# Two transformer blocks in one kernel: bias tables and a norm's squares moved beside weight chunks, and the modulated operand made by three engines

## The reference

```python
mod = jax.nn.silu(c) @ w_ada[l] + b_ada[l]
shift, scale, gate = jnp.split(mod[:, None, :], 3, axis=-1)
h = rms_norm(x, norm_g[l]) * (1.0 + scale) + shift          # hc likewise, from ctx and c_ctx
(a_glu, a_gate, nq, nk, nv, n_gate, wq, wk, wv, w_gate, merge) = jnp.split(h @ w_in[l], SPLIT_POINTS, axis=-1)
# convolution branch: depthwise convolution of 31 taps, layer norm over 512 channels, silu
# neighbourhood attention with a relative bias table (na_rpb), window attention with a sink
x = x + gate * (sum of three gated branches) @ w_o
```

## Time and profile before

| what | value |
|---|---|
| median of three runs | 2804.88 us |
| profiled execution, its own time | 2804.84 us |
| its span | 2803.1 us |
| PE busy | 2529.4 us, 90% |
| VectorE busy | 1530.3 us, 55% |
| ScalarE busy | 1274.4 us, 45% |
| GpSimd busy | 219.6 us, 8% |
| mean granted clock of TensorE | 0.927 of full speed |

### The profile page before, as it was taken

The page is one execution under the profiler, slowest core; times in us unless marked ns, Lnnn a source line. Parts: engine busy times, 40 slices in busy tenths (PEclk is TensorE's granted clock), DMA queues, the critical chain, the costliest instruction groups (busy, mean ns, idle before and its releaser), DMA issues. The chain is left out here.

```text
span 2803.1 us, 46994 instructions
## 1 busy us (share of the span) xinstructions
PE 2529.4 (90%) x17866; PEld 2276.6 (81%) x17866; DVE 1530.3 (55%) x2701; ACT 1274.4 (45%) x1969; POOL 219.6 (8%) x212
## 2 busy tenths in 40 slices
PE   6897679999889689959998999899999989898998
PEld 4676458887678579949996879899999977798998
DVE  4488553334558555625556555555555454655554
ACT  5364553232546454414345454543443454544433
POOL 0022000000003000002100000022021000000220
PEclk8999899999989799979996789999999976999999
DMA  8221022222532025435532214455355432153552
GB/s 333 103 94 45 14 91 91 91 104 90 210 120 95 24 91 185 176 114 183 190 140 101 96 70 180 141 184 186 136 187 187 142 128 76 67 190 136 179 180 105
DMA packets 60996, 368.56 MB, mean 131 GB/s; under 512 B 5888, under 2 KB 18224, under 8 KB 18352
## 3 DMA queue, kind: packets, MB, share of 16 engines
q1 hardware_dynamic: 60704, 366.49, 36.5%
q10 hardware_dynamic: 144, 0.01, 0.0%
HBM read 359.10 MB, written 7.37 MB: 131 GB/s over the span
## 5 line engine op out<-in xcount | busy, mean ns | idle before, releaser
L210 DVE TENSOR_TENSOR w_lo<-ring,w_hi 128x1024 fp32r<-128x1024 f32 x652 | 819.9, 1299 | 547.0 <-ACT w_hi L198 547.0
L252 PE MATMUL psum<-x_hi,w_hi 128*128 128x256 f32 (+1 forms) x3392 | 1041.0, 307 | 66.4 <-DVE x_lo L570 21.9
L253 PE MATMUL psum<-x_lo,w_hi 128*128 128x256 f32 (+1 forms) x3392 | 1032.0, 304 | 0.0
L254 PE MATMUL psum<-x_hi,w_lo 128*128 128x256 f32 (+1 forms) x3392 | 1031.5, 304 | 0.0
L198 ACT ACTIVATE w_hi<-ring 128x1024 fp32r<-128x1024 f32 (+1 forms) x652 | 653.4, 1050 | 356.3 <-PE psum L254 154.2
L252 PEld LDWEIGHTS psum<-x_hi,w_hi 128*128 128x128 f32 x3392 | 659.3, 194 | 103.1 <-issue 58.4
L253 PEld LDWEIGHTS psum<-x_lo,w_hi 128*128 128x128 f32 x3392 | 659.8, 195 | 24.0 <-issue 1.4
L254 PEld LDWEIGHTS psum<-x_hi,w_lo 128*128 128x128 f32 x3392 | 659.3, 194 | 23.3
L1553 PE MATMUL psum<-h_hi,w_hi 128*128 (+1 forms) x640 | 181.1, 283 | 0.0
L1555 PE MATMUL psum<-h_lo,w_hi 128*128 (+1 forms) x640 | 181.1, 283 | 0.0
L1556 PE MATMUL psum<-h_hi,w_lo 128*128 (+1 forms) x640 | 181.1, 283 | 0.0
(11 more groups left out here) (275 smaller groups left out, 3202.6 us busy)
## 6 DMA issues: line engine op xcount, KB each, us to landing
ring<-wstream SPq DMA_DIRECT2D x327, 1024.0 KB, 4.8
kept_hi<-x_hi SPq DMA_DIRECT2D x1, 2048.0 KB, 6.3
kept_lo<-x_lo SPq DMA_DIRECT2D x1, 2048.0 KB, 13.0
x_hi<-kept_hi SPq DMA_DIRECT2D x1, 2048.0 KB, 7.8
x_lo<-kept_lo SPq DMA_DIRECT2D x1, 2048.0 KB, 12.5
near<-bias_by_distance SPq DMA_DIRECT2D x2, 1024.0 KB, 7.5
na_bias<-rpb SPq DMA_DIRECT2D x4, 438.0 KB, 5.7
cst<-consts SPq DMA_DIRECT2D x1, 1662.0 KB, 10.5
```

The source lines that it names most:

```text
L210: dve.tensor_tensor(w_lo[:, c % 2, h], ring[:, (c + 2 * i) % RING, h], w_hi[:, c % 2, h].bitcast(F32), ALU.subtract).then_inc(split_done.s ...
L252: pe.matmul(o, w_hi[:, c, w_cols], hi, start=first, stop=False)
L253: pe.matmul(o, w_hi[:, c, w_cols], lo, start=False, stop=False)
L254: return pe.matmul(o, w_lo[:, c, w_cols], hi, start=False, stop=last)
```

## The change

The new parts, by stage:

- `ada_stage`: its loops are written out. ScalarE squares x two tiles at a time beside chunks 8 to 11, and PE sums them a chunk later, into another bank of psum. In layer 0 x and the context are loaded behind chunks 2 and 3 of the loop, the vectors and constants behind 5 and 6, block 2's table and buckets behind 7.
- `mod_stage`: takes the inverse root and multiplies x by it (128x512). In layer 0 it also makes the product of table and buckets and writes it to memory.
- `model_norm`: ScalarE scales and shifts (two activations a tile), GpSimd rounds 128x512, VectorE subtracts 128x512. The first glu chunk is worked through with both tiles side by side.
- `conv_norm_stage` takes the place of `halve_stage` with `norm_of` and of the bias stage in `attend_near`: one stage, with the bias table requested at its head.
- `merge_stage` of the last layer splits x into the right half of x_hi and x_lo beside the out chunks (`halves`).
- `RelBias` in the first `ffn_stage`: the table is read at its head, six flips stand behind chunk 1 and two behind chunk 3. The read of the compressed keys' part falls away, it is taken from the flipped table.

```diff
-        def mod_stage(mod, rows, layer):
+        def mod_stage(mod, rows, layer, scratch, tables):
...
+                    if layer == 0:
+                        sp.wait_ge(read.sem, read.n + 2)
+                        sp.dma_start(table, tables[2][:]).then_inc(loaded.sem, 16)
+                        sp.wait_ge(loaded.sem, lb + 16)
...
+                    if layer == 0:
+                        pe.matmul(psum[0:2 * HEADS, 2048:2048 + 511], tables[0][:], tables[1][:], start=True, stop=True
+                                  ).then_inc(read.sem, 1)
...
+                    inverse_root(act, psum[:, 1024:1024 + 2 * S], rs[:], eps_col, r0)
...
+                    dve.wait_ge(rooted.sem, r0 + 2)
+                    for k in range(KT):
+                        dve.tensor_tensor(scratch(k), x[:, k, :], rs[:], ALU.mult).then_inc(scaled_x.sem, 1)
...
                     for j in range(n):
                         load_one(sp, j // 2, j % 2)
+                        if j == 2:
+                            sp.dma_start(x[:, :, 0:S], xT).then_inc(stored.sem, 16)
+                        if j == 3:
+                            sp.dma_start(x[:, :, S:2 * S], ctxT).then_inc(stored.sem, 16)
+                        if j == 5:
+                            sp.dma_start(vec[:], vecs).then_inc(loaded.sem, 16)
                         if j == 6:
-                            sp.dma_start(vec[:], vecs).then_inc(loaded.sem, 16)
+                            sp.dma_start(cst[:], consts[:, 0:N_RESIDENT]).then_inc(loaded.sem, 16)
...
-                    each_chunk(pe, n, chunk)
+                    for j in range(n):
+                        chunk(j // 2, j % 2)
+                        for k in range(2 * (j - first - 1), 2 * (j - first)):
+                            if k >= 0:
+                                sum_squares(pe, k)
+                    for k in range(2 * (n - first - 1), KT):
+                        mm = sum_squares(pe, k)
...
+                        for k in range(2 * (j - first), 2 * (j - first) + 2):
+                            if k >= 0:
+                                act.activation(scratch(k), x[:, k, :], ACT.Square).then_inc(squared.sem, 1)
...
             def act_steps(act):
                 for k in range(KT):
+                    act.wait_ge(scaled_x.sem, s0 - KT + k + 1)
+                    for w in range(2):
+                        v = scratch(k)[:, w * S:w * S + S]
+                        o = act.activation(v, v, ACT.Identity, scale=scales[:, k, w:w + 1], bias=mod[:, k, w:w + 1])
+                    o.then_inc(mixed.sem, 1)
+                round_next(act, 0, 0)
+
+            def pool_steps(pool):
                 for k in range(KT):
+                    pool.wait_ge(mixed.sem, m0 + k + 1)
+                    pool.tensor_copy(x_hi[:, k, :], scratch(k)).then_inc(upper.sem, 1)
...
+                for k in range(KT):
+                    dve.wait_ge(upper.sem, u0 + k + 1)
+                    dve.tensor_tensor(x_lo[:, k, :], scratch(k), x_hi[:, k, :].bitcast(F32), ALU.subtract
+                                      ).then_inc(lower.sem, 1)
                 rest_next(dve, 0, 0)
...
+        def conv_norm_stage(layer, tok, src, scratch, na_bias, jobs):
...
+                    for k in range(nt):
+                        mm = pe.matmul(psum[:, 0:tok], ones, src[:, k, 0:tok], start=k == 0, stop=k == nt - 1)
+                    mm.then_inc(step.sem, 1)
+                    pe.wait_ge(loaded.sem, lb + 32)
+                    for h in range(6):
+                        mm = turn_round(h)
+                    mm.then_inc(parted.sem, 1)
+                    for k in range(nt):
+                        pe.wait_ge(squared.sem, q0 + k + 1)
+                        mm = pe.matmul(psum[:, 512:512 + tok], ones, scratch[:, k, 0:tok], start=k == 0,
+                                       stop=k == nt - 1)
+                    mm.then_inc(step.sem, 1)
+                    for h in range(6, HEADS):
+                        pe.wait_ge(mixed.sem, m0 + h - 5)
+                        mm = turn_round(h)
+                    mm.then_inc(parted.sem, 1)
...
+                    dve.wait_ge(rooted.sem, r0 + 2)
+                    for k in range(nt):
+                        dve.tensor_tensor(src[:, k, 0:tok], src[:, k, 0:tok], rs[:, 0:tok], ALU.mult
+                                          ).then_inc(scaled_x.sem, 1)
+                    lower_part(1)
+                    dve.wait_ge(parted.sem, f0 + 2)
+                    for h in range(6, HEADS):
+                        bias_of(h)
+                    dve.memset(na_bias[:, NA_COLS:], 0.0)
...
+            def x_upper(act, j, i):
+                m = slice(2 * i, 2 * i + 2)
+                act.wait_ge(acc_free.sem, g0[0] + j)
+                act.activation(x_hi[:, m, S:], x[:, m, 0:S], ACT.Copy).then_inc(upper.sem, 1)
...
+        class RelBias:
...
+            def pe(self, pe, part):
+                pe.wait_ge(loaded.sem, self.lb + 32)
+                for k in (range(6), range(6, 8))[part]:
+                    if part:
+                        pe.wait_ge(mixed.sem, self.m0 + k - 5)
+                    mm = pe.matmul(self.bank(k), const("flip"), rel_bias[:, 2 * k:2 * k + 2, :], start=True, stop=True)
+                mm.then_inc(parted.sem, 1)
...
-        rel_bias_stage()
-        split_stage(x[:, :, 0:S], x_hi[:, :, 0:S], x_lo[:, :, 0:S])
         for layer in range(DEPTH):
-            ffn_stage(layer, layer_norm(layer - 1, 3) if layer else None)
+            ffn_stage(layer, layer_norm(layer - 1, 3) if layer else None, bias=None if layer else RelBias())
```

More of the change, by code:

```diff
@@ L355, in _ @@
                     mm.then_inc(step.sem, 1)
+                    if layer == 0:
+                        pe.matmul(psum[0:2 * HEADS, 2048:2048 + 511], tables[0][:], tables[1][:], start=True, stop=True
+                                  ).then_inc(read.sem, 1)
+                @block.scalar
+                def _(act):
+                    inverse_root(act, psum[:, 1024:1024 + 2 * S], rs[:], eps_col, r0)
+                    if layer == 0:
+                        act.wait_ge(read.sem, read.n + 1)
+                        act.activation(tables[2][:], psum[0:2 * HEADS, 2048:2048 + 511], ACT.Copy).then_inc(read.sem, 1)
                 @block.vector
@@ L369, in _, with ada_stage @@
                                               None, ALU.mult)
-            step.n += 3
-        def ada_stage(c_both, rows, layer):
+                    dve.wait_ge(step.sem, b + 2)
+                    dve.tensor_tensor(mod[:], v[:, :, 2:4], mod[:], ALU.add).then_inc(step.sem, 1)
+                    dve.wait_ge(step.sem, b + 3)
+                    dve.scalar_tensor_tensor(out=scales[:], in0=mod[:, KT:2 * KT, :], scalar=1.0,
+                                             in1=par(layer, "norm_g").unsqueeze(2).to_broadcast([P, KT, 2]),
+                                             op0=ALU.add, op1=ALU.mult)
+                    dve.wait_ge(rooted.sem, r0 + 2)
+                    for k in range(KT):
+                        dve.tensor_tensor(scratch(k), x[:, k, :], rs[:], ALU.mult).then_inc(scaled_x.sem, 1)
+            step.n += 3
+            rooted.n += 2
+            scaled_x.n += KT
+            if layer == 0:
+                read.n += 2
+                loaded.n += 16
+        def ada_stage(c_both, rows, layer, scratch, tables):
             n = ADA_CHUNKS
             b = step.n
+            q0, x_loaded = squared.n, stored.n + (32 if layer == 0 else 0)
+            first = 8
             with nc.Block() as block:
@@ L577, in layer_norm @@
             return Norm(None, act_steps, dve_steps, lambda pe, k: pe.wait_ge(lower.sem, l0 + k + 1))
-        def split_stage(src, hi, lo):
-            b = step.n
-            with nc.Block() as block:
-                @block.scalar
-                def _(act):
-                    act.activation(hi, src, ACT.Copy).then_inc(step.sem, 1)
-                @block.vector
-                def _(dve):
-                    dve.wait_ge(step.sem, b + 1)
-                    dve.tensor_tensor(lo, src, hi.bitcast(F32), ALU.subtract).then_inc(step.sem, 1)
-            step.n += 2
@@ L912, in _ @@
                                                ).then_inc(upper.sem, 1)
+                        if halves and kind == "out" and i:
+                            x_upper(act, j, i - 1)
                         if kind in ("gate", "merge"):
@@ L988, in _ @@
                                 y_lower(2, slice(6, 8))
+                        if halves and kind == "out" and i:
+                            x_lower(dve, i - 1)
                         if kind == "out":
                             take_out(dve, j, i)
+                    if halves:
+                        x_lower(dve, OUT_CHUNKS - 1)
                     if moments:
@@ L1112, in _ @@
                     pool.memset(cpad[:, :, :, PAD + S:], 0.0)
+                    norm.pool(pool)
                 @block.vector
@@ L1486, in ffn_stage @@
```

(14 more changed lines are left out.)

427 lines of the change are left out of this document (184 added, 243 removed).

## The result

The changed kernel takes 2723.66 us (median of four runs, 2719.38 to 2729.70); the kernel before ran beside it at 2805.70 (four runs, 2802.95 to 2808.51). The ratio is 0.9709 (0.9685 to 0.9734), so 82 us less; forecast were 76.5. The profiled execution took 2719.38 us, 85.5 less than the one before. Five more runs, in another session (last experiment), gave 2736.05 (ratio 0.9753). Both lie within the range, and the difference between the sessions is explained under "the hardware".

The account below looks back on a forecast made before the run. PE, busy 90% of the span, bounds the kernel, so gains come only where it stands still. Terms 34.3 + 25.5 + 10.2 + 6.5 = 76.5 us took 2804.8 to 2728 us; range 2712 to 2744.

Parts of the forecast that it names:

- between the blocks: Between block 1 and block 2: removing the table and rounding stage saves 41.5 us, flips cost 7.2, net 34.3 us.
- convolution norm and near bias: From the convolution's norm to near attention: requesting the bias table at stage opening saves 12.2 and 13.3 us, together 25.5.
- norm, layer 0: Norm ahead of layer 0's first projection: first glu chunk ends at 81.2 instead of 91.4, saving 10.2 us (6 to 14).
- norm, layer 1: Norm ahead of layer 1's first projection: chunk 1 starts at 787.1 instead of 793.6, saving 6.5 us (2 to 10).
- Rival (c): In the ffn, tables land late or VectorE's adds starve PE: up to 10 us wait at chunk 2, 2738 us; chance 0.05.
- with the same bytes in all; so I expect chunk 12 near 50 ... and the last two sums until 55.5: Layer 0's ada stage: reordered loads bring chunk 12 near 50, sums end at 55.5, block opens at 56, 2.4 us later.
- on the loads if layer 0's transposes start after 58: Sign in layer 0's norm: transposes starting after 58 would show the forecast wrong on the loads.
- ada of layer 1 should be some 3 us longer up to chunk 11: Sign in layer 1's ada stage: it should take some 3 us longer up to chunk 11.
- a step is 0.7 + 0.69 + 0.05 = 1.45: In the norms: GpSimd's round and VectorE's subtract cannot overlap, so each step takes 1.45 us; bounds 0.91 and 4.3.
- What a step costs: In the norms: GpSimd and VectorE lock each other out of a shared port, so a step is their sum, 1.45 us.
- Rival (d): In the norms: GpSimd's round beside VectorE makes the kernel slower, losing 76.5 us at 6.2 us a step; chance 0.02.
- Rival (b): Whole kernel: more is won, with no GpSimd and VectorE hindrance, early loads, warm PE: 88 us, 2717 us; chance 0.11.

Follow-up runs that it names:

- last experiment: The changed kernel run once more unchanged (e11), beside another run of e6's kernel on one chip: 2736.05 us against 2717.43 us.
- e4: Changed kernel with the stage between the blocks (bias tables, flips, adds, split of x) put back: 2758.24 us.
- e7: Changed kernel with the convolution's norm and the neighbourhood bias in two stages again, table requested at the head of the second: 2750.54 us.
- e1: Changed kernel with the loads of block 2's table and buckets on a count of their own: 2725.92 us, ratio 0.9711.
- e2: Kernel before the change, with only the ada stages' hardware loops written out: 2796.86 us, ratio 0.9974.
- e10: Changed kernel with each of GpSimd's rounds made twice, one after the other: 2737.85 us, one run.
- e9: Changed kernel with the multiplies by the root between VectorE's subtracts and the root in psum: 2722.15 us, one run.
- e3: Changed kernel with the norm's operand made as before by VectorE and ScalarE in 256 columns, GpSimd idle: 2721.61 us.
- e5: Changed kernel with multiplies between VectorE's subtracts, table loads counted apart and SyncE's wait for the written table moved to RelBias: 2719.92 us.
- e11: The changed kernel once more, nothing different, in another session: 2736.05 us, ratio 0.9753.
- e6: Changed kernel with the operand by VectorE and ScalarE, table loads counted apart and SyncE's wait for the written table moved: 2715.47 us.

## Why the prediction was right, step by step

| term | forecast | measured |
|---|---|---|
| between the blocks | 34.3 | 43.3 - 6.9 = 36.4 in the profile; 34.6 by e4 |
| convolution norm and near bias | 25.5 | 13.3 + 14.2 = 27.5 in the profile, 26.4 of them in the stage itself; 26.9 by e7 |
| norm, layer 0 | 10.2 | 3.7 |
| norm, layer 1 | 6.5 | 13.4 |
| not in any term | 0 | 4.5, of which 3.9 are one stage of block 2 at another clock |

**Between the blocks**: right. One rounding and one subtract after the last take_out took until 1148.65, and PE began at 1149.12, 1.9 us after the take_out ended; I had 1.8. Chunk 0 took 6.0 us instead of the 7.8 that I kept from the slow clock, and that is the surplus. It is partly luck: in e1, with the same instructions there, chunk 0 took 7.5 at a granted clock of 0.82. The length before also varies, 52.06 us in its profile and 48.35 in e2, so the term is 32.7 to 36.4. The flips cost 6.9 (forecast 7.2). VectorE's adds were hidden: chunk 3's split began at 1169.65, and chunks 2 and 3 are read 5.76 us apart. Rival (c) did not come.

**Convolution norm**: right. Layer 0's table landed 7.1 us after its request, 0.85 after the sums. In layer 1 PE waited 4.92 for it, as I had said.

**Norm, layer 0**: the step "with the same bytes in all; so I expect chunk 12 near 50 ... and the last two sums until 55.5" failed, and not in its first half, since chunk 12 is rounded at 50.43. I counted bytes and did not ask what the first sums wait for. They wait for all four small loads, the bucket's among them, which landed 10.5 us after its issue. The block opened at 64.05 instead of 56: 5.5 of these 8.05 us are that wait, for without it the root starts at 58.55 (e1). Most of the rest is seen in e1 too: 3.60 us of sums behind the last chunk, four tiles, where I had two. My sign for it, "on the loads if layer 0's transposes start after 58", showed (64.07). From root to read it took 23.8 us, where I had 25.2.

**Norm, layer 1**: undersized by 6.9 us, in two terms of about the same size: the block opened 3.5 us earlier after the last take_out than I had, and root to read was 3.2 us shorter. I set the loops' unrolling against a table load and so at nothing; the chunks now come in pairs of 5.0 us where the hardware loop needed 5.65, and e2 measures 3.0 us for it. So my sign "ada of layer 1 should be some 3 us longer up to chunk 11" failed: it was 0.4 longer. And "a step is 0.7 + 0.69 + 0.05 = 1.45" was 1.01; from the first subtract's end to the last one's were 7.4 us, where seven steps of 1.45 are 10.2, so 2.7 less. The bound beside that term was mis-added as well: with steps of 0.91 its own sum gives 10.3, not 9.6.

**What a step costs**: the mechanism, exclusion, was right, the size was wrong. A cast alone took 0.61 us (I took 0.7), a subtract alone 0.69, but 0.14 and 0.15 us of these are beginning and end, which may overlap with the other; exclusive are 0.47 and 0.54. The Trainium skill, in "SBUF — State Buffer", section "SBUF: two separate sides", says that the two block each other fully, each for the whole instruction, and share no bandwidth. The traces agree but for the 0.14 us at the ends: every subtract that begins within a cast ends 0.54 us after it, e10's second cast puts 0.56 on every step, and with an input of psum (e9) nothing is blocked. In the changed kernel the exclusion costs little, since ScalarE's 0.98 a tile (I had 0.91) would pace the steps without it. What the changed kernel loses to two engines (e3, 2.2 us a layer) is the order, eight multiplies ahead of everything else; the price of the exclusion shows where the order is mended, 2.2 us between e5 and e9. Rival (d) was far off, since no cast took over 1.1 us; nor was any as long as the 1.4 that I gave for one beside a subtract.

The two norm terms were 16.7 together and came out at 17.1, by two errors that cancel. The total says nothing of either, and that it came out so near is in this part luck. Rival (b) had the two large terms almost exactly (36 and 28) and overrated the norms (24). My "about 0.2% (5.6 us)" for what a measurement can tell was too small: two medians of the changed kernel lie 12.4 us apart.

## What to carry to other kernels

When loads move to another place, look up for each what counts it and who waits for that count: an early consumer that waits for a shared count waits for the last load in it. A stage worth moving is one in which PE stands for a transfer or for one short operation; put beside weight chunks, it costs only its matmuls (7 us of 52 here). Before handing half of a VectorE step to GpSimd, see which VectorE instructions beside it have two SBUF inputs: add the exclusive parts, and compare with one engine alone. Where one of these inputs can lie in psum, that instruction leaves the sum; with it, and with the multiplies between the subtracts, three engines gave the shortest norm of all (15.07 us in layer 1, e9), but in one run only.

## What the runs showed of the hardware

The same stage of block 2 (265 matmuls, nothing of the change in it) takes 42.24, 38.37 and 46.07 us in the profiles of before, after and e11, with a granted clock of 0.72, 0.82 and 0.59 (windows, one of each execution):

```profile
1632.50:1674.74 42.24, 36.49 (x265) 25.29 (x264) 26.61 (x145) 26.54 (x86) 0.00 (x0) 0.72 0.04 10
```

```profile
1550.88:1589.25 38.37, 32.13 (x265) 22.54 (x264) 26.28 (x145) 26.84 (x85) 0.00 (x0) 0.82 0.05 12
```

```profile
1551.45:1597.52 46.07, 41.81 (x265) 28.65 (x264) 26.93 (x145) 26.23 (x86) 0.00 (x0) 0.59 0.04 10
```

The last two are the same kernel. PE is idle for 4 to 6 us of this stage, in short waits for the attention's softmax steps on VectorE and ScalarE, and how much of it runs at the slower of the two levels (1.2 GHz) differs from one execution to the next. That is 7.7 us, the larger part of the 10.8 between these two executions, while their last take_out is at 1146.39 and 1146.85. Why the second session kept to the slow pattern in all five runs stays open. Block 1 varies in the same way. Here are 65 us of layer 0's attention, between the same two instructions, in after and in e6:

```profile
289.12:353.95 64.83, 47.41 (x420) 35.70 (x422) 42.07 (x161) 41.15 (x99) 0.00 (x0) 0.84 0.17 66
```

```profile
282.30:349.20 66.90, 49.44 (x420) 37.20 (x422) 42.27 (x161) 41.14 (x98) 0.00 (x0) 0.78 0.16 64
```

The end of layer 0's merge takes 32.5 us in after (granted clock 1.00) and 35.2 in e6 (0.90). This is not the work of e6's edit: e4, whose code up to there is that of after, takes 67.05 and 35.20 us for the two stretches, at 0.78 and 0.90. So an execution can take back some 5 us of what an edit won ahead of it. Edits of 2 to 6 us are therefore read from stretches here, and not from medians.

A cast of 128x512 from f32 takes 0.61 us on GpSimd and 0.42 on VectorE. A read of 64 KB that was issued between weight loads landed after 10.5 us.
